# Expert layer in the split form: three rounded products of 176 columns in place of one fp32 product

## The reference, cut to what matters

```python
def swiglu(h, wg, wu, wd):
    return (jax.nn.silu(h @ wg) * (h @ wu)) @ wd

def moe(h, w_router, wg, wu, wd):
    probs = jax.nn.softmax((h @ w_router).astype(F32), -1)
    top_p, top_i = lax.top_k(probs, TOP_K)            # TOP_K = 2 of N_EXPERTS = 8
    top_p = top_p / jnp.sum(top_p, -1, keepdims=True)
    gates = jnp.sum(jax.nn.one_hot(top_i, N_EXPERTS, dtype=F32) * top_p[..., None], -2)
    out = jnp.zeros_like(h)
    for e in range(N_EXPERTS):                        # wg, wu: (1024, 1408), wd: (1408, 1024)
        out = out + gates[..., e:e + 1] * swiglu(h, wg[e], wu[e], wd[e])
    return out
```

## Time and profile before

| | |
|---|---|
| median of the runs (lowest to highest) | 2539.14 us (2539.13 to 2541.26) |
| profiled execution: its time, its span | 2534.16 us, 2532.5 us |
| mean granted TensorE clock | 0.902 |
| TensorE matmuls busy | 2220.1 us, 88% of the span |
| VectorE, ScalarE, GpSimd busy | 766.9, 468.4, 249.1 us |
| DMA | 306.00 MB, mean 121 GB/s |
| expert loop, first to last product | 1814.6 to 2483 us |

### The profile page before, as it was taken

One profiled execution on the slowest core, in us unless ns is written; L12 is line 12 of the kernel. 1 busy time (PEld: TensorE's weight loads), 2 busy tenths in 40 slices (PEclk: granted clock), 3 DMA queues, 4 the chain that ended last, 5 costly groups with the idle time before them and its releaser, 6 DMA issues.

```text
span 2532.5 us, 33729 instructions
## 1 busy us (share of the span) xinstructions
PE 2220.1 (88%) x13726; PEld 2007.2 (79%) x13726; DVE 766.9 (30%) x1437; ACT 468.4 (18%) x1020; POOL 249.1 (10%) x332
## 2 busy tenths in 40 slices
PE   5899898976769999997898699997699999999992
PEld 4788787864659999996754577776699999999992
DVE  2245555537232222222224366721100000000003
ACT  1133422203022212211123200101201111111101
POOL 0000101020002302300110033200100000000001
PEclk8899999956789999998898689987799999999996
DMA  7222100030213242342060245520788988898883
GB/s 193 67 67 75 36 1 4 1 95 26 83 34 92 72 113 76 88 113 62 29 231 1 67 166 223 193 75 0 197 217 214 272 208 210 210 273 211 210 204 124
DMA packets 452944, 306.00 MB, mean 121 GB/s; under 512 B 22382, under 2 KB 435457, under 8 KB 448705
## 3 DMA queue, kind: packets, MB, share of 16 engines
q1 hardware_dynamic: 433812, 225.74, 34.0%
q0 software_dynamic: 19024, 78.72, 9.1%
HBM read 276.42 MB, written 28.14 MB: 120 GB/s over the span
## 4 chain that ended last, share of the span: by engine, by line
PE 67%; issue 19%; DVE 6%; POOL 4%; DMA 2%; SPq 1%; ACT 1%; POOLq 0%; DVEq 0%; ACTq 0%
PE bank L1156 17%; PE bank L510 13%; PE bank L1185 8%; PE bank L1062 6%; POOL actL L2194 2%; PE bank L690 2%; PE bank L675 1%; PE bank L685 1%; PE bank L1079 1%; PE bank L548 1%; POOL actH L2191 1%; SPq L2303 1%; PE bank L841 1%; PE bank L845 1%; PE bank L843 1%
## 5 line engine op out<-in xcount | busy, mean ns | idle before, releaser
L1156 PE MATMUL bank<-arena,w_ring 128*128 128x176 f32 x2816 | 424.5, 314 | 4.6 <-issue 4.6
L1156 PEld LDWEIGHTS bank<-arena,w_ring 128*128 128x128 f32 x2816 | 422.4, 191 | 6.6 <-issue 6.6
L510 PE MATMUL bank<-hT,w_ring 128*128 128x260 f32 x1600 | 364.0, 390 | 16.3 <-DVE hT L1208 15.1
L510 PEld LDWEIGHTS bank<-hT,w_ring 128*128 128x128 f32 x1600 | 310.1, 194 | 66.4 <-DVE hT L1208 16.0
L1185 PE MATMUL bank<-arena 128*128 128x176 f32 x1408 | 219.6, 313 | 0.0
L1185 PEld LDWEIGHTS bank<-arena 128*128 128x128 f32 x1408 | 210.2, 190 | 0.0
L1777 ACT ACTIVATE arena<-bank 128x512 f32<-128x512 f32 (+4 forms) x200 | 86.7, 454 | 421.8 <-PE bank L510 226.3
L1739 DVE TENSOR_TENSOR arena<-arena,bank 128x176 f32<-128x176 f32 x88 | 29.7, 337 | 431.4 <-PE bank L1156 431.4
L841 PE MATMUL bank<-hH,gu_high 128*128 128x260 f32 x704 | 142.7, 284 | 18.1 <-DVE w_low L1467 18.1
L1062 PE MATMUL bank<-arena 128*128 128x256 f32 x640 | 151.0, 387 | 3.9 <-DVE arena L1597 3.9
L845 PE MATMUL bank<-hH,w_low 128*128 128x260 f32 x704 | 142.5, 284 | 0.0
(11 more groups left out here) (438 smaller groups left out, 2824.7 us busy)
## 6 DMA issues: line engine op xcount, KB each, us to landing
w_ring<-in_we_gate SPq DMA_DIRECT2D x88, 512.0 KB, 7.2
w_ring<-in_we_up SPq DMA_DIRECT2D x88, 512.0 KB, 7.3
arena<-in_we_down SPq DMA_DIRECT2D x64, 704.0 KB, 6.4
w_ring<-in_w_in_a SPq DMA_DIRECT2D x26, 512.0 KB, 3.7
w_ring<-in_w_gate SPq DMA_DIRECT2D x22, 512.0 KB, 3.8
w_ring<-in_w_up SPq DMA_DIRECT2D x22, 512.0 KB, 3.8
arena<-in_w_down SPq DMA_DIRECT2D x16, 704.0 KB, 6.2
slots<-arena POOLq DMA_DIRECT2D x4, 2560.0 KB, 21.8
```

The source lines that it names most:

```text
L510: mm = pe.matmul(out[i][:, 0:hi - lo], w_ring[:, s, kt, :], rhs[:, kt, lo:hi], start=(kt == 0), stop=(kt == KT - 1))
L1156: mm = pe.matmul(bank[bk][:, 0:SLOTS], w_ring[:, s, kt, :], hTe[:, kt, :], start=(kt == 0), stop=(kt == KT - 1))
```

## The change

The expert loop goes over to the split form. Weight blocks are split on ScalarE and VectorE, four blocks ahead of their use, into a ring of five high tiles (over the space of xT and hT) and, for the low part, in place over the raw weights. Tokens and activations are split too. Each fp32 matmul becomes three float32r matmuls. The weight loads become 256 columns wide (1 MB for a gate or up pair, 1.375 MB for a down pair), into six pair slots and three down slots; the results go through a ring of four tiles, and the last results of a pass are copied out by VectorE and ScalarE early in the next one. New semaphore `high_free` counts finished blocks.

```diff
+EX_SLOTS, EX_DOWN, EX_HIGH, EX_OUT = 6, 3, 5, 4
+EX_AHEAD = 4
...
+        def gu_load(m):
+            f, up = m // 2, m % 2
+            return (2 * (f // 2) + up, f % 2) if f < 2 * EX_PAIRS else (2 * EX_PAIRS, up)
...
 # TensorE
+            def expert_product(out, low, top, x_low, x_high, first, last, slot_used):
+                mm = pe.matmul(out[:, 0:SLOTS], low, x_high, start=first, stop=False)
+                if slot_used is not None:
+                    mm.then_inc(slot_used, 1)
+                pe.matmul(out[:, 0:SLOTS], top, x_low, start=False, stop=False)
+                mm = pe.matmul(out[:, 0:SLOTS], top, x_high, start=False, stop=last)
+                if last:
+                    mm.then_inc(high_free, 1)
...
-                        pe.wait_ge(w_loaded[s], p * 32 + 16 * (w0[s] + r + 1))
+                        pe.wait_ge(split, p * BLOCKS + split0 + m + 1)
                         pe.wait_ge(bank_free[bk], p * per[bk] + f0[bk] + f // 2)
                         for kt in range(KT):
-                            mm = pe.matmul(bank[bk][:, 0:SLOTS], w_ring[:, s, kt, :], hTe[:, kt, :],
-                                           start=(kt == 0), stop=(kt == KT - 1))
-                        mm.then_inc(w_used[s], 1)
+                            expert_product(bank[bk], low[:, kt, :], top[:, kt, :], ehL[:, kt, :], ehH[:, kt, :], kt == 0, kt == KT - 1,
+                                           w_used[j % EX_SLOTS] if half and kt == KT - 1 else None)
...
                         for f in range(FB):
-                            mm = pe.matmul(bank[bk][:, 0:SLOTS], d_ring[:, s, f * P:(f + 1) * P], acte[:, f, :],
-                                           start=(f == 0), stop=(f == FB - 1))
+                            if i == 0:
+                                pe.wait_ge(act_split, p * FB + loops["act0"] + f + 1)
+                            expert_product(bank[bk], low[:, f, :], top[:, f, :], eactL[:, f, :], eactH[:, f, :], f == 0, f == FB - 1,
+                                           d_used[j % EX_DOWN] if half and f == FB - 1 else None)
...
 # VectorE: low part of block m; multiply; tokens' low part; results
+                    def low_part(m):
+                        raw_block, low, top = expert_parts(m)
+                        dve.wait_ge(high, p * BLOCKS + split0 + m + 1)
+                        dve.tensor_tensor(low, raw_block, top.bitcast(F32), ALU.subtract).then_inc(split, 1)
+                    low_part(0)
+                    low_part(1)
+                    with dve.If(p > 0):
+                        block_out(p, KT - 1, back=1)
...
+                    for m in range(BLOCKS):
+                        if m + EX_AHEAD < BLOCKS:
+                            low_part(m + EX_AHEAD)
...
+                        if m == 2 * FB - 1:
+                            for g in range(4):
+                                dve.wait_ge(h_high, p * 4 + KT + 4 + g + 1)
+                                dve.tensor_tensor(ehL[...], bank[6 + g % 2][:, 0:2 * SLOTS], ehH[...].bitcast(F32), ALU.subtract)\
+                                   .then_inc(bank_free[6 + g % 2], 1)
...
 # ScalarE: high part of block m
+                        act.wait_ge(high_free, p * BLOCKS + m + 1)
+                        act.activation(top, raw_block, ACT.Copy).then_inc(high, 1)
...
 # GpSimd: activations
+                    for f in range(FB):
+                        bu = 2 + f % 2
+                        pool.wait_ge(bank_free[bu], p * per[bu] + f0[bu] + f // 2 + 1)
+                        pool.tensor_tensor(eactH[:, f, :], sge[:, f % 2, :], ones[:, 0:1].to_broadcast([P, SLOTS]), ALU.mult)\
+                            .then_inc(pool_step, 1)
+                        pool.wait_ge(pool_step, p * FB + 2 * FB * DENSE_PARTS + f + 1)
+                        pool.tensor_tensor(eactL[:, f, :], sge[:, f % 2, :], eactH[:, f, :].bitcast(F32), ALU.subtract)\
+                            .then_inc(act_split, 1)
...
 # SP
+                        if j < 2 * EX_PAIRS:
+                            lo = j // 2 * 2 * P
+                            load(dst, columns("we_up" if j % 2 else "we_gate", lo, lo + 2 * P), w_loaded[s])
...
+                        load(down_slots[s][0], columns("we_down", j * 2 * P, (j + 1) * 2 * P), d_loaded[s])
```

More of the change, by code:

```diff
@@ L283, in build, with both @@
         htok, _ = place(q, 5, D)
-        acte, q = place(q, FB, SLOTS)
+        eactH, q = placed("eactH", q, FB, SLOTS)
+        eactL, q = placed("eactL", q, FB, SLOTS)
+        ehH, q = placed("ehH", q, KT, SLOTS)
+        ehL, q = placed("ehL", q, KT, SLOTS)
         sge, q = place(q, 2, SLOTS)
-        yTe, q = place(q, KT, SLOTS)
         yrow, q = place(q, 2, D)
-        hTe, q = place(q, KT, SLOTS)
         hrow, q = place(q, 2, D)
+        def both(name, shape, over, at):
+            return (nc.alloc_sbuf_tensor_at(name, [P] + shape, F32, offset=base[over] + at)[:],
+                    nc.alloc_sbuf_tensor_at(name + "_low", [P] + shape, F32R, offset=base[over] + at)[:])
+        pair = KT * 2 * P * 4
+        gu_at = [("w_ring", i * pair) for i in range(EX_SLOTS - 1)] + [("memkT", 0)]
+        gu_slots = [both(f"gu_pair{i}", [KT, 2 * P], over, at) for i, (over, at) in enumerate(gu_at)]
+        down_slots = [both(f"down_pair{i}", [FB, 2 * P], "arena", q + i * FB * 2 * P * 4) for i in range(EX_DOWN)]
+        assert q % 32 == 0 and q + EX_DOWN * FB * 2 * P * 4 <= arena_bytes
+        ex_high = [rounded(f"ex_high{i}", [FB * P], "xT", i * FB * P * 4) for i in range(EX_HIGH)]
+        yTe = nc.alloc_sbuf_tensor_at("yTe", [P, EX_OUT, SLOTS], F32, offset=base["xT"] + EX_HIGH * FB * P * 4)[:]
+        assert EX_HIGH * FB * P + EX_OUT * SLOTS <= 2 * KT * T and base["hT"] == base["xT"] + KT * T * 4
         mq1, q = place(0, 2, T)
@@ L887, in _ @@
             loops["parts"] = 0
+            loops["act0"] = 2 * FB * DENSE_PARTS + 1
             memory_attention(0)
@@ L1746, in _ @@
+            block_out(n_passes, KT - 1, back=1)
             dve.wait_ge(gfin_in, 16)
@@ L2085, in _ @@
                 with act.If(p < n_passes):
[L2086 to L2102, removed]
+                    def high_part(m):
+                        raw_block, _, top = expert_parts(m)
+                        expert_loaded(act, p, m)
+                        act.wait_ge(high_free, p * BLOCKS + m + 1)
+                        act.activation(top, raw_block, ACT.Copy).then_inc(high, 1)
@@ new lines, in _ @@
+                    for m in range(EX_AHEAD):
+                        high_part(m)
+                    with act.If(p > 0):
+                        for i in range(KT - 2, KT):
+                            rows_of_block(p, i, back=1)
+                    for m in range(BLOCKS):
+                        if m + EX_AHEAD < BLOCKS:
+                            high_part(m + EX_AHEAD)
+                        if m < 2 * FB and m % 2 == 0:
+                            f = m // 2
+                            expert_done(act, p, m)
+                            act.wait_ge(act_split, p * FB + loops["act0"] + f - 1)
+                            act.activation(sge[:, f % 2, :], bank[f % 2][:, 0:SLOTS], ACT.Silu).then_inc(bank_free[f % 2], 1)
+                        if m == 2 * FB - 1:
+                            for g in range(4):
+                                act.wait_ge(hx, p * 4 + 4 + g + 1)
+                                act.activation(ehH[:, 2 * g:2 * g + 2, :].rearrange("p a b -> p (a b)"), bank[6 + g % 2][:, 0:2 * SLOTS],
+                                               ACT.Copy).then_inc(h_high, 1)
+                            act.wait_ge(rows_out, p * 16 + 16 * ZFILL)
+                        if m >= 2 * FB + 2:
+                            rows_of_block(p, m - 2 * FB - 2)
@@ L2103, in _ @@
+            for i in range(KT - 2, KT):
+                rows_of_block(n_passes, i, back=1)
             for t in range(NT + 1):
```

133 lines of the change are left out of this document (95 added, 38 removed).

## The result

The changed kernel takes 3294.49 us (median of 4 runs, 3290.14 to 3294.91) against 2539.14: ratio 1.2974, 95% interval 1.2952 to 1.2997. The direction was as predicted; the size was not. 137 us more were forecast, it is 755. The profiled execution took 3294.91 us with a span of 3293.3.

A forecast was written before the change was run, and what follows sets the result against it. TensorE's instruction stream was taken to bound the kernel. Products and token transposes over 8 passes plus the start, 8 x (16.0 + 0.8) + 3 = 137.4 us on the median 2539.14, gave 2677 us, range 2605 to 2710.

The forecast's parts named there:

- The bound now: Expert loop before the change: TensorE's instruction stream binds, fp32 records 149.9 ns apart, 79.1 us of products a pass; weights come in time.
- The price of a rounded product: Expert loop products: 120.1 ns each as in the dense layer, 792 a pass, 95.1 us against 79.1, +16.0 us a pass.
- D: Rival, much slower: products streamed twice (2865 us), or waits or a halved clock at pass borders (2715 to 2780); chance 0.08.
- rival C: Faster: in the expert loop only columns bind, 75.8 ns a product, 2412 us; chance 0.05.
- rival B: Only the weight load binds in the expert loop, 107 to 112 ns a product, 2593 to 2625 us; chance 0.26.
- A: The predicted case: whatever holds 260-column products at 120 ns, such as the instruction feed, holds 176 there too; 2677 us, chance 0.60.
- Splitting weights and activations: Splits on ScalarE (some 43 us a pass), VectorE (49) and GpSimd (at most 20) run beside the products and cost nothing.
- Token transposes: Banks of the third and fourth token group come free later, after a VectorE subtraction: +0.8 us a pass, between 0 and 2.
- Loads: Same bytes, 65 us of a pass of 100; next pass's loads behind the fourth down load still come in time: nothing.
- Results: VectorE copies the last down block after two low parts, still in time; the 1.2 us at the pass end stay.
- Start: Before the loop's first product, the first block must be rounded and subtracted: +3 us once, between 1 and 8.

The follow-up runs named there:

- e2: The changed kernel with each three rounded products replaced by one fp32 matmul of raw weights with the tokens' high part: 2632.76 us.
- e1: The changed kernel with products 256 columns wide instead of 176, except in each block's last tile and the first down block: 2723.3 us, ratio 1.0749.
- e5: The changed kernel, still 176 columns, with result copies before splits and the next pass's first four blocks split during this pass's last four: 3272.77 us.
- e7: As e5, with products 224 columns wide in place of 176: 2632.7 us.
- e8: As e5, with the two high-weight products joined into one matmul of 352 columns, two weight loads a tile instead of three: 2559.66 us, ratio 1.0091.
- e6: As e5, with only the first six gate and up blocks of each pass 224 columns wide, the others 176: 2730.47 us.
- e11: As e10, with products 184 columns wide: 2699.63 us.
- e10: The changed kernel in the order of e5, products 200 columns wide except in each block's last tile and the first down block: 2634.18 us.

## Why the prediction was wrong

**The bound now.** Right: TensorE's stream bounded the kernel, at 149.9 ns a record, and e2 has the same spacing. One reading was weaker than it looked: that rounded products stream their columns once was read from 215 to 220 ns at half clock, which is also the pace of a load there (213.3). e1 shows it: 256 columns stand 118 ns apart at full clock, where twice their number would take 213.

**The price of a rounded product.** This is the step that failed, twice over. First, "a rounded product of any width takes some 107 to 112 ns", or 120.1 as sustained in the dense layer: both are prices at full clock, and I took the clock of the old loop for granted. It wasn't a property of the loop but of its products. The old fp32 records stream 352 columns for one load, longer than the load at either clock (146.7 against 112 ns, 293 against 213); the dense layer's 260 columns are as long as a load at half clock (216.7 against 213 ns). With 176 columns the load binds at either clock, and the full clock was never granted. Price: 213.3 ns, 80 us of the 94.7 a pass. A halved clock in the loop stood in the prediction only as what would make it wrong, and among the rivals as short falls at pass borders (D, 2715 to 2780), which the runs with wide columns did show, but not as a state of the whole loop. The rows for it were there: half-clock rounded products in the earlier trace rows, loads of up to 337 ns in the earlier trace rows. Working out the price at either clock, and asking at which of them TensorE would settle, would have made it a rival with a number: 8 x (792 x 0.2133 - 79.1) = 719 us more.

The Trainium skill, "TensorE: Matmul & The Clock Gate", section "Why this matters for your kernels", has TensorE reach the full clock by being kept busy and lose it in gaps between bursts. The trace has it at half clock while busy 98% of the time, and e5, with the waits for results gone, is no different: here the measurement decides against the rule as a sufficient one. The price that the prediction takes from the section "Back-to-back issue gap" (75.8 ns, the source of rival C) is given there as the gap of a single matmul, and the section itself says that with few columns it is too low where a weight load goes with each; with 176 columns the runs have 112 ns.

Second, at full clock rival B was right and A wrong. Products of 176, 184, 200 and 224 columns all stand 111 to 112 ns apart when the clock is full: the floor of L1125, not the feed's 120. 256 columns take 118 and the dense layer's 260 take 120, so that number grows with the columns once they come near the load. What adds 8 to 10 ns there is open; that no feed of 120 ns for every product binds is shown by the 112. Had the clock been full and nothing else gone wrong, 792 x 0.112 = 88.7 us is the term, +9.6 a pass. A's argument failed in one sentence: "in the dense layer load and columns are each under 112 ns, and yet it takes 120" was taken for a third limit that holds at any width.

**Splitting weights and activations.** Busy times right: VectorE 51 us a pass (forecast 49), ScalarE 43 (43), GpSimd 13 (at most 20). "Cost nothing" counted busy time and block pace, and was wrong by the order in front of the results.

**Token transposes.** Forecast +0.8 us, between 0 and 2. The wait for VectorE's token parts is 0.5 us a pass here and 1.1 us in e2 at full clock; right.

**Loads.** "On SP the loads of the next pass now stand behind the fourth down load" looked at the next pass's loads and not at who waits for the fourth itself: 6.6 us to land, then two splits, and behind them the result copies. Missed.

**Results.** "The 1.2 us at the pass end stay as they are" was wrong: VectorE's low parts of the next pass wait for ScalarE's high parts, the first of which starts 1.9 us after TensorE's result transposes at the border (2004.0 to 2005.9 in e2). 1.28 us of this is the table load shown above. The trace of the changed kernel has two in each pass, one ahead of the first rounding (2169.11) and one ahead of the first SiLU (2182.20); before there was one, ahead of the SiLU. The last result is copied at 2009.3. Both waits with the rest are the 97 us of e2, 12 a pass. In the changed kernel itself the half clock hid most of it.

**Start.** +3 forecast (1 to 8), 5.9 measured: within bounds. The trace has the 1.28 us load of ScalarE's table ahead of the first rounding here too (1816.78), which I hadn't counted.

So of the 755 us, about 640 are the clock (8 x 80.2), 77 the weight-load floor (8 x 9.6), and the last 36 the order, transposes at half clock and the start. That split is worked out from spacings; what was measured as a whole is 3272.8 against 2632.7 us for 176 and 224 columns in the same order and on the same chip, 640 us.

## What to carry to other kernels

Price a TensorE instruction at both clocks and for both of its parts, load and columns. Where the load outlasts the columns, don't take the full clock for granted (TensorE was busy for 98% of the loop at half clock), and try some more columns. Where one stationary operand serves two products, put their moving operands side by side: one load less for each three took 73 us here (2632.7 to 2559.7 us, e7 to e8), and with two more waits gone it was 2489.7. Before a stage is split across three engines, list for each in-order engine what stands in front of the operation that TensorE waits for.

## What the runs showed of the hardware

- Eight columns more (184 instead of 176, in the same order) made the kernel 573 us faster (3272.8 to 2699.6, one run each): at the one width the full clock came, after 127 us, at the other it never did.
- The same 176-column products were seen at either clock, by what went before: at full clock for 80 us at a stretch behind wider ones that had been granted it (e6), at half clock for 1430 us where it hadn't been granted.
- A weight load of 128 columns of rounded weights sets a pace of 111 to 112 ns at full clock (176 to 224 columns streamed) and 213.3 at half (176 and 184).
- Behind a wait of some 2 us of TensorE the clock fell in six of eight passes among 176-column blocks (e6), in two of seven with 184 columns (e11), in one of eight with 224 (e7) and in none with 200 (e10). What decides it from pass to pass, with nothing different in the program, no run here shows.
- ScalarE loaded a function table for 1.28 us twice in each pass of the changed kernel, ahead of the first rounding copy and of the first SiLU, and once before.
